# The samples' attention written out step by step, its value products one step later, its first cache loads and new rows' scores moved into the last prompt head

## The reference

```python
ckv_past = cache_ckv[page_table].reshape(dbsz, past_len, KV_LORA)      # 8 samples x 4096 rows x 256
kpe_past = cache_kpe[page_table].reshape(dbsz, past_len, QK_ROPE)      # 8 samples x 4096 rows x 64
...
s = concat([scores(ckv_past, kpe_past), scores(ckv_new, kpe_new)])     # 8 heads, scaled
p = softmax(s)
o = einsum('bhqk,bkr->bqhr', p[..., :n_past], ckv_past) + einsum('bhqk,bkr->bqhr', p[..., n_past:], ckv_new)
```

## Time and profile before

| | us |
|---|---|
| median of 3 runs | 2642.34 |
| lowest and highest of them | 2637.77 and 2643.88 |
| the profiled execution's own time | 2639.37 |
| span of the profile | 2637.5 |
| the samples' stage in it, from the last prompt value product to the first projection product | 1370.1 to 1698.6 |

### The profile page before, as it was taken

How to read it: one execution, slowest core, us unless ns; L and a number is a source line. 1 busy time by engine, 2 the same in 40 slices (tenths; PEclk the granted TensorE clock), 3 DMA queues, 4 the chain that set the end, 5 groups by cost and what they waited for, 6 DMA issues and landing times.

```text
span 2637.5 us, 36344 instructions
## 1 busy us (share of the span) xinstructions
PE 2426.4 (92%) x14022; PEld 2210.0 (84%) x14022; DVE 1291.1 (49%) x2467; ACT 770.4 (29%) x1469; POOL 361.7 (14%) x308
## 2 busy tenths in 40 slices
PE   7799999999999678999988888898999999999994
PEld 7799999999999578889876666687999989899993
DVE  4623343433333855777757777644244333333336
ACT  2331111111111324555546555412311111111112
POOL 2400000000000411000016555033000000000006
PEclk9899999999999889999999999899999999999997
DMA  4111111111111031000015444411211111101111
GB/s 156 33 57 47 48 48 48 39 33 40 48 48 41 20 122 41 18 18 11 1 32 168 139 132 150 162 40 32 65 49 48 39 41 48 49 19 47 48 41 64
DMA packets 137064, 153.72 MB, mean 58 GB/s; under 512 B 10256, under 2 KB 114224, under 8 KB 136808
## 3 DMA queue, kind: packets, MB, share of 16 engines
q1 hardware_dynamic: 124656, 110.07, 13.3%
q0 software_dynamic: 12288, 41.95, 5.0%
HBM read 142.24 MB, written 10.32 MB: 58 GB/s over the span
## 4 chain that ended last, share of the span: by engine, by line
PE 79%; DVE 9%; issue 4%; ACT 3%; POOL 3%; DMA 2%; SPq 0%; POOLq 0%; DVEq 0%; ACTq 0%
PE ps L214 23%; PE ps L216 22%; PE ps L215 22%; DVE split L207 4%; PE ps L2000 2%; ACT split L202 2%; PE ps L2035 2%; POOL plain L338 1%; POOL plain L340 1%; PE ps L222 1%; PE ps L221 1%; PE ps L2015 1%; PE ps L1543 1%; PE ps L2016 1%; DVE plain L290 1%
## 5 line engine op out<-in xcount | busy, mean ns | idle before, releaser
L214 PE MATMUL ps<-split 128*128 128x512 f32 (+6 forms) x3632 | 1244.9, 343 | 71.7 <-DVE split L207 22.9
L215 PE MATMUL ps<-split 128*128 128x512 f32 (+6 forms) x3632 | 1229.3, 338 | 0.0
L216 PE MATMUL ps<-split 128*128 128x512 f32 (+6 forms) x3632 | 1228.4, 338 | 0.0
L214 PEld LDWEIGHTS ps<-split 128*128 128x128 f32 x3632 | 695.2, 191 | 121.9 <-issue 31.2
L216 PEld LDWEIGHTS ps<-split 128*128 128x128 f32 x3632 | 695.4, 191 | 37.9
L215 PEld LDWEIGHTS ps<-split 128*128 128x128 f32 x3632 | 695.4, 191 | 36.6
L202 ACT ACTIVATE split<-plain 128x1024 fp32r<-128x1024 f32 (+8 forms) x446 | 313.5, 738 | 623.5 <-PE ps L222 405.8
L207 DVE TENSOR_TENSOR split<-plain,split 128x1024 fp32r<-128x1024 f32 (+7 forms) x422 | 355.5, 867 | 187.6 <-ACT split L202 181.7
L274 DVE TENSOR_TENSOR plain<-plain,ps 128x512 f32<-128x512 f32 (+2 forms) x396 | 268.3, 684 | 201.7 <-PE ps L216 196.3
L910 DVE TENSOR_TENSOR plain<-plain,ps 128x350 f32<-128x350 f32 (+1 forms) x132 | 68.0, 515 | 585.7 <-ACT plain L866 585.2
L207 DVE TENSOR_TENSOR split<-ps,split 128x512 fp32r<-128x512 f32 (+5 forms) x480 | 246.4, 554 | 173.8 <-ACT split L202 171.1
(11 more groups left out here) (145 smaller groups left out, 1440.6 us busy)
## 6 DMA issues: line engine op xcount, KB each, us to landing
plain<-w_gate SPq DMA_DIRECT2D x44, 512.0 KB, 4.6
plain<-w_up SPq DMA_DIRECT2D x44, 512.0 KB, 4.0
plain<-w_down SPq DMA_DIRECT2D x44, 512.0 KB, 4.2
plain<-x_prompt SPq DMA_DIRECT2D x8, 512.0 KB, 11.3
x_spill<-plain SPq DMA_DIRECT2D x1, 4096.0 KB, 18.1
plain<-wo SPq DMA_DIRECT2D x8, 512.0 KB, 4.8
plain<-x_spill SPq DMA_DIRECT2D x8, 512.0 KB, 7.8
y_prompt<-plain SPq DMA_DIRECT2D x8, 512.0 KB
```

Source lines behind the costliest of these rows:

```text
L214: pe.matmul(out, still[0], moving[0], start=start, stop=False)
L215: pe.matmul(out, still[0], moving[1], start=False, stop=False)
L216: return pe.matmul(out, still[1], moving[0], start=False, stop=stop)
```

## The change

- decode_steps is one list of steps without a loop, on PE, ACT, DVE, and so are the loads on POOL and the small DMAs on SP. Tests for a loop variable (isinstance) go.
- LAG = 3: the values are three steps behind the key turn, so in step c of sample b it is chunk c-3 of sample b-1, or chunk c+5 of sample b-2 in steps 0 to 2. Sample 9 has 5 steps instead of 4. split_outputs follows.
- DVE's output sums move from step 2, behind the key parts, to step 3, ahead of the key parts. turn_output, late and what DVE does behind them move from step 3 to step 4.
- new_scores goes into the last head, at the end of its step 1, and writes bank 2; DVE copies the result at the head of step 2, and the scores of the last block wait for that copy.
- POOL issues the loads of chunks 0 and 1 once head 7's queries and weights are there, clears the buffers once all head units are done, and waits for the last turn of the last head before chunk 2. It no longer waits for the last scores and values. The waits for the end of the last head stand in decode_pe ahead of the first step, as new_scores had them.

```diff
+    def new_scores():
+        pe.wait_ge(s["sq_taken"], 6 * (k.heads // 2))
+        for b in range(k.ns):
+            for m in range(3):
+                rows = slice(0, 64 if m == 2 else P)
+                mm = pe.matmul(k.ps[0:1, 2, 8 * b:8 * b + 8], k.lat_s[rows, m, b:b + 1], k.q_all[rows, :, m, b],
+                               start=m == 0, stop=m == 2)
+        mm.then_inc(s["small"], 1)
...
+        if m == 8 * k.heads - 1:
+            pe.wait_ge(s["new_s"], 1)
...
         placed_units(h, n, LATE)
+        if h == k.heads - 1 and n == 1:
+            new_scores()
...
+        if h == k.heads - 1 and n == 2:
+            dve.wait_ge(s["small"], 1)
+            dve.wait_ge(s["qp_steps"], 2 * k.heads)
+            dve.tensor_copy(k.new_s, k.ps[0:1, 2, 0:64]).then_inc(s["new_s"], 1)
         if h < k.heads:
             row_max(m)
...
-CHUNKS = 8
+CHUNKS, LAG = 8, 3
...
-def decode_steps(eng, step):
-    for c in range(CHUNKS):
-        step(0, 0, c, True, c >= 1, False)
-    for c in range(CHUNKS):
-        step(1, 1, c, True, True, c >= 2)
-    with eng.Fori(1, 4) as j:
-        for par in range(2):
-            for c in range(CHUNKS):
-                step(2 * j + par, par, c, True, True, True)
+def decode_steps(step):
+    for b in range(8):
+        for c in range(CHUNKS):
+            step(b, b % 2, c, True, b > 0 or c >= 1, b > 1 or (b == 1 and c >= LAG))
     for c in range(CHUNKS):
         step(8, 0, c, False, c == 0, True)
-    for c in range(4):
-        step(9, 1, c, False, False, c < 2)
+    for c in range(LAG + 2):
+        step(9, 1, c, False, False, c < LAG)
...
+    pool.wait_ge(s["block_ready"], 4)
     pool.wait_ge(s["own_w_lo"], 2 * k.heads)
-    pool.wait_ge(s["qp_lo"], 2 * k.heads)
+    pool.wait_ge(s["wr_lo"], k.heads // 2)
+    pool.wait_ge(s["wv_lo"], k.heads // 2)
     pool.wait_ge(s["sq_done"], k.heads)
     pool.wait_ge(s["sq_taken"], 6 * (k.heads // 2))
-    pool.wait_ge(s["filled"], FILLS_BEFORE[8 * k.heads])
-    pool.wait_ge(s["pv_done"], 4 * k.heads)
-    pool.wait_ge(s["s_done"], 8 * k.heads)
-    pool.wait_ge(s["block_ready"], 4)
+    for u in range(2):
+        load(u)
+    pool.wait_ge(s["hd_unit_done"], len(k.unit_no))
+    pool.wait_ge(s["qp_lo"], 2 * k.heads)
     pool.memset(k.band_q.bitcast(F32), 0.0).then_inc(s["band_zero"], 1)
     pool.memset(k.max_col, 0.0).then_inc(s["band_zero"], 1)
     pool.memset(k.xt_tail.bitcast(F32), 0.0).then_inc(s["band_zero"], 1)
...
+    pool.wait_ge(s["filled"], FILLS_BEFORE[8 * k.heads])
+    for u in range(2, k.ns * CHUNKS):
+        load(u)
...
 def before_value(b, c):
-    vb, vc = (b - 1, c - 2) if c >= 2 else (b - 2, c + 6)
+    vb, vc = (b - 1, c - LAG) if c >= LAG else (b - 2, c + CHUNKS - LAG)
...
-        if c == 3 and output_of(b):
+        if c == 4 and output_of(b):
             turn_output(b - 2)
-        if c == 3 and softmax_of(b):
+        if c == 4 and softmax_of(b):
             late(b - 1)
...
 # decode_dve: the five output sums, ahead of the key parts of step 3
+        if c == LAG and output_of(b):
+            dve.wait_ge(s["dpv_done"], CHUNKS * (b - 1))
...
         if keys:
             key_lo(0)
...
-        if c == 2 and output_of(b):
-            dve.wait_ge(s["dpv_done"], CHUNKS * (b - 1))
...
-        if c == 3 and output_of(b):
+        if c == 4 and output_of(b):
             dve.wait_ge(s["out_turned"], b - 1)
...
-        if c == 3 and softmax_of(b):
+        if c == 4 and softmax_of(b):
             dve.wait_ge(s["small"], 1 + 3 * (b - 1) + 3)
```

More of the change, by code:

```diff
@@ L1916, in output_of @@
 def output_of(b):
-    return not isinstance(b, int) or 2 <= b <= 9
+    return 2 <= b <= 9
 def decode_sp(sp, k):
@@ L1928, in decode_sp @@
     sp.dma_start(k.ckv_new, k.ckv_sample[0]).then_inc(s["new_in"], 16)
-    with sp.Fori(1, 8) as b:
+    for b in range(1, 8):
         sp.wait_ge(s["late_taken"], 2 * b)
-        sp.dma_start(k.ckv_new, k.ckv_sample[bass.ds(b, 1), 0, :]).then_inc(s["new_in"], 16)
+        sp.dma_start(k.ckv_new, k.ckv_sample[b:b + 1, 0, :]).then_inc(s["new_in"], 16)
     sp.wait_ge(s["dc_lo"], k.ns * CHUNKS)
@@ L1952, in decode_pool @@
     pool.memset(k.xt_tail.bitcast(F32), 0.0).then_inc(s["band_zero"], 1)
-    def load(b, c):
-        u = CHUNKS * b + c
-        if not isinstance(b, int) or u >= 4:
-            pool.wait_ge(s["dc_lo"], u - 3)
-        row = k.block_now[:, c % 4:c % 4 + 1]
-        pool.tensor_copy(row, k.block[:, bass.ds(u, 1)]).then_inc(s["block_copied"], 1)
-        pool.wait_ge(s["block_copied"], u + 1)
-        wait_apart(pool, k)
-        for src, dst in ((ckv, k.cache_raw(c % 4)[:, 0:1024]), (kpe, k.cache_raw(c % 4)[:, 1024:1280])):
-            pool.indirect_dma_start(dst, None, src, bass.IndirectOffsetOnAxis(row, 0))\
-                .then_inc(s["cache_in%d" % (c % 4)], 16)
-    for c in range(CHUNKS):
-        load(0, c)
-    with pool.Fori(1, 8) as b:
-        for c in range(CHUNKS):
-            load(b, c)
+    pool.wait_ge(s["filled"], FILLS_BEFORE[8 * k.heads])
+    for u in range(2, k.ns * CHUNKS):
+        load(u)
 def key_part(k, u_c, m):
@@ L2037, in values @@
         mm.then_inc(s["dpv_done"], 1)
-    def new_scores():
-        pe.wait_ge(s["sq_taken"], 6 * (k.heads // 2))
-        pe.wait_ge(s["exp_done"], 8 * k.heads)
-        pe.wait_ge(s["pt_lo"], RUNS_BEFORE[FILLS_BEFORE[8 * k.heads]])
-        pe.wait_ge(s["o_copied"], 4 * k.heads)
-        pe.wait_ge(s["band_zero"], 3)
-        for b in range(k.ns):
-            for m in range(3):
-                rows = slice(0, 64 if m == 2 else P)
-                mm = pe.matmul(k.ps[0:1, SMALL_BANK, 8 * b:8 * b + 8], k.lat_s[rows, m, b:b + 1], k.q_all[rows, :, m, b],
-                               start=m == 0, stop=m == 2)
-        mm.then_inc(s["small"], 1)
     def small(b, n):
@@ L2093, in output_of_late @@
     def output_of_late(b):
[L2094 removed]
+        return b >= 1
     def turn_output(b):
@@ L2120, in step @@
             max_spread(b - 1)
-        if c == 3 and output_of(b):
+        if c == 4 and output_of(b):
             turn_output(b - 2)
-        if c == 3 and softmax_of(b):
+        if c == 4 and softmax_of(b):
             late(b - 1)
-    decode_steps(pe, step)
+    decode_steps(step)
     pe.wait_ge(s["out_taken"], k.ns)
@@ L2191, in decode_act @@
     act.wait_ge(s["sq_taken"], 6 * (k.heads // 2))
-    decode_steps(act, step)
+    decode_steps(step)
 def decode_dve(dve, k):
@@ L2202, in key_lo, with add @@
             lo_part(dve, lo, src, hi).then_inc(s["kt_lo"], 1)
+        if c == LAG and output_of(b):
+            dve.wait_ge(s["dpv_done"], CHUNKS * (b - 1))
+            ps = k.ps[:, VALUE_BANK, :]
+            dve.wait_ge(s["late_taken"], 2 * (b - 1))
+            base = 4 * (b - 2)
+            rows = k.out_rows
+            def add(part, n):
+                dve.wait_ge(s["do_steps"], base + n)
+                return dve.tensor_tensor(rows, rows, part, ALU.add)
+            dve.tensor_tensor(rows, k.new_out, ps[0:8, 0:256], ALU.add).then_inc(s["do_steps"], 1)
+            add(ps[0:8, 256:512], 1).then_inc(s["do_steps"], 1)
+            add(ps[64:72, 0:256], 2).then_inc(s["do_steps"], 1)
+            add(ps[64:72, 256:512], 3).then_inc(s["do_steps"], 1)
+            dve.wait_ge(s["do_steps"], base + 4)
+            dve.tensor_scalar(rows, rows, k.sum_inv, None, ALU.mult).then_inc(s["out_norm"], 1)
         if keys:
@@ L2270, in step @@
         split_outputs(k, dve, b, c, False)
-    dve.wait_ge(s["small"], 1)
-    dve.tensor_copy(k.new_s, k.ps[0:1, SMALL_BANK, 0:64]).then_inc(s["new_s"], 1)
-    dve.wait_ge(s["new_s"], 1)
-    decode_steps(dve, step)
+    decode_steps(step)
 def samples_operand(dve, k):
```

58 lines of the change are left out of this document (28 added, 30 removed).

## The result

The changed kernel takes 2608.40 us (median of 4 runs, 2604.51 to 2611.03) where the kernel before, beside it, took 2640.54 (4 runs): a ratio of 0.987, 95% interval 0.9853 to 0.9886. It is faster by 1.3%, some 32 us where 22 were forecast. The forecast time, 2617, was 8.6 too high; the measured one lies at the very low end of the range. The profiled execution took 2611.03 us, against 2639.37 before, 28.3 less.

A forecast was written before the change was run, and what follows sets the result against it. PE's wait for DVE's output sums in samples 2 to 7, with the clock drop behind it, and the samples' start were taken to bound the kernel. 8 + 14.4 + 1.0 - 1.1 = 22.3 us off 2639.4 gave 2617, range 2608 to 2631.

The forecast's parts named there:

- V(2): PE's four value products of step 2, samples 2 to 7: start without waiting for DVE's output sums, taking 1.0 us.
- T(3): PE's ten transposes of chunk 3: last part waits for a key split, from about 1567.0 to 1568.0.
- V(3): PE's four value products of step 3: a second wait, 1.8 us, for DVE's output sums.
- T(4): PE's ten transposes of chunk 4, samples 2 to 7: follow V(3), at 1572.6 in the sample read.
- T(5): PE's ten transposes of chunk 5: start at 1577.8 instead of 1580.22, so 2.4 us gained per sample.
- Rival 1: Samples 2 to 7: PE's clock falls in the new waits too, costing about 10 us in all: 2627; chance 0.20.
- rival 2: Samples 2 to 7: the stall goes altogether, giving 16.5 us more: 2600; chance 0.05.
- rival 3: Samples 2 to 7: fetching the written-out straight code stops the path, 9 fetches costing 41 us: 2658; chance 0.04.
- From there POOL paces as before.: First sample from chunk 4's load, started 7.4 us earlier: POOL's queue sets the same pace as before.
- I charge them in full, 2.54: New rows' scores in head 7, on PE's path: cost 2.54 us, bounds 0 to 2.54 plus DVE's copy of 0.2.
- rival 4: Start gives little: DVE blocked by POOL in head 7, 5.2 us lost: 2622; chance 0.05.
- T(0): PE's ten transposes of chunk 0, at the samples' start: 1373.0 instead of 1379.13, 6.1 us earlier.

The follow-up runs named there:

- e7: Kernel before with 128 semaphore instructions added at the head of PE's own code: 2634.22 us, ratio 0.9983.
- e6: Changed kernel with the separate semaphore instruction put back between POOL's index copy and the indirect transfer: 2606.84 us, ratio 0.9885 to the kernel before.
- e2: Kernel before with its three loops over samples written out as straight code, nothing else changed: 2634.77 us, ratio 0.9979.
- e3: Kernel before with POOL's load loop written out and without its separate semaphore instruction before the indirect transfer: 2635.12 us, ratio 0.9982.
- e10: e7 profiled once more, the kernel before with 128 padding instructions on PE: 2635.49 us in one run.
- e4: Changed kernel with POOL's three clears moved behind its wait for the last fill of the head: 2604.03 us, ratio 0.9862 to the kernel before.
- e8: Changed kernel, step 2 reordered: probabilities' high and low parts behind the key parts, output sums at its end: 2596.16 us, ratio 0.9848 to the kernel before.
- e11: e8 with e4's later POOL clears, without padding: 2597.01 us, ratio 0.9825 to the kernel before.

## Why the prediction was right and where it went wrong

Right was the mechanism in samples 2 to 7, step by step: V(2) without a wait, the eviction behind it, T(3) idle 0.87 (1.0 was said), V(3) idle 1.69 (1.8), T(3) to T(4) 6.4 (6.3), T(4) to T(5) 5.05 (5.2), the clock at 1.00. The period is 34.4 where 34.7 was said. The size was a little off: 16.8 us instead of 14.4. The periods of before less those after are 2.5 to 2.9 in five of the samples, where 2.4 had been read from one, and 3.4 in the last, where the kernel before happened to be at half clock for 6.8 us; against e7 the gain would be 14.3. So these profiles cannot tell whether 14.4 was too small. The rule that the clock holds up to 1.65 and falls from 2.38 of idle on was a bad guide, though its answer was right: PE stayed at 2.4 GHz behind 2.20 (e6) and, in sample 7 of e7, 3.61, and fell behind 1.93 (ahead of T(8) in e2) and 1.02 (e3). Rival 1 (the clock falls) fell with the window at 1.00, rival 2 (the stall goes altogether) with the two waits, and rival 3 (straight code) with e2.

Wrong were these steps; the two profiles differ by 28.3 us where 22.3 were forecast.
- *"Outside that stage and the last prompt head the change moves nothing."* The second FFN's stretch is 6.0 us shorter, with not a line of it changed (774.8 to 768.9): three edges of its loop cost 4.7 us of idle where two pairs had cost 7.8, and by its granted clock PE was at 1.2 GHz for 18 us of the stretch instead of 24, which is worth the other 3. This term was put at nothing without a reason, and it is the largest part of what was missed; its rows ("issue", 7.8 us) were there to be asked about.
- *"From there POOL paces as before."* It did not: each load is 0.54 us shorter without the separate semaphore instruction, a removed line of the diff to which the sum gave no term. Sample 0 gained 5.8, not 1.9; POOL's part alone gave it 3.5 (e3), and taking the change of POOL's line back cost 4.7 (e6). Sample 1 gained 2.1 instead of 1.0, but against the 31.9 of e7 and e10 it gained 0.6 to 1.2, near the forecast.
- *"I charge them in full, 2.54"* and, of POOL's work in head 7, *"I take 0".* The scores cost some 4.3 with the clock that they bring down, DVE was the loser against POOL's clears, and both together lengthened the head by 6.5. So rival 4's mechanism was true, at 2.2 to 2.9 us beside the scores (44.8 to 47.1 or 47.7) rather than 5.2. By the Trainium skill, page "SBUF — State Buffer", section "SBUF: two separate sides", whichever of the two starts first gets the shared port pair and the other fully blocks. That DVE is the one blocked agrees with 2.27 us against 0.30; that the first to start wins doesn't show in the rows, where DVE's operation starts 0.69 us ahead of the first clear, and no run tells the port from another cause. T(0) gained 1.8 instead of 6.1. Since sample 0 gave back what this lost, the start as a whole came to 7.6 against a forecast of 8: right by two errors that cancel.
- The tail lost 0.7 in one profile and 2.1 in the other, where 1.1 was said.
- Two slips in the working: T(0) at 1373.0 plus the 5.2 to the value split gives 1378.2 for chunk 4, not 1377.8, and the terms' own bounds give 2613 to 2622, not 2612 to 2624. The sum doesn't move with them.

The terms missed thus are 6.0 for the loop's edges, 2.4 and 1.1 in the samples (both in part the clock of the one execution of before), and -0.4 at the start; a tail 0.4 better and the rest of the last stretch, 0.5 worse, cancel. Against them stand 3.1 us by which the profiled execution's first 1330 us were longer, in code that is the same. With the 22.3 that makes 28.3 us; the difference of the medians, 32 us, is near the sum without the 3.1, but nothing shows that this is the reason.

## What to carry to other kernels

Give each removed line of a diff its own term, the ones that look like bookkeeping too: on a queue that sets the pace, 0.54 us an item came to some 4 us in one sample. Work moved into a stage to lie "under" it has to be weighed against what it holds up on other engines there and what it does to the clock, not only by its own duration. And before a small gain is put down to an edit, look at a stretch that the edit doesn't touch, and profile the unchanged kernel twice: here a loop that no edit touched took 761.6 to 774.9 us, depending on what else the program held, the idle behind its edges was gone with 64 or 128 idle instructions ahead of all, and the same samples took 217.6 and 223.1 us in the same program.

## What the runs showed of the hardware that I had not expected

- A DVE tensor_scalar on 128x144 that takes 0.30 us took 2.27 beside three POOL clears, ending 0.1 us behind the last of them.
- 48 small products in 2.54 us, without idle, were followed by a fall of PE's clock to 1.2 GHz for 3.4 us (e4); an idle of 2.98 us went with one of 6.8 (after). In the same head e3 had one of 3.4 with neither.
- The same wait of 3.6 to 3.7 us in samples 2 to 7 of the old order was followed by 3.4 us at 1.2 GHz (most samples), by 6.8 (sample 7 of before, all six of e2) or by none (sample 7 of e3 and e7).
- Each of three edges of the FFN's loop either costs 1.3 to 2.0 us of idle (3.4 to 4.4 in a pair) and 9 instruction packets, or nothing; which of them do was the same in a second profile of two kernels, and differs with code on other engines (e8 and e11).
- A semaphore instruction of its own between a POOL copy and the indirect transfer that uses it lengthens the gap from 0.27 to 0.81 us (e6); at the head of PE's code such an instruction takes 0.16 us at most (128 of them, 20.6 us).
